# Attention's second projection moved to the end of its step, and VectorE's late copy moved ahead of the second maximum

## What is computed

```
dq = rope(rms_norm(dq.reshape(B, T, DA_HEADS, 2, DA_DK), lp['g_qn']), pos)
dk = rope(rms_norm(dk.reshape(B, T, DA_HEADS, 2, DA_DK), lp['g_kn']), pos)
s = einsum('bqhmd,bkhmd->bhmqk', q, k) * (DA_DK ** -0.5)      # two maps m per head
p = softmax(where(mask, s, min))
a = p[:, :, 0] - lam * p[:, :, 1]
o_d = rms_norm(einsum('bhqk,bkhe->bqhe', a, v), lp['g_dnorm']) * (1.0 - lam_init)
```

## Time and profile before

| | |
|---|---|
| median of 3 runs | 2151.39 us (2151.34 to 2151.40) |
| the profiled execution: its time | 2156.33 us |
| its span | 2154.5 us |
| TensorE busy | 2142.9 us, 99% |
| VectorE busy | 1161.8 us, 54% |
| ScalarE busy | 846.9 us, 39% |
| GpSimd busy | 505.6 us, 23% |
| attention loop | about 480 to 1037 us from the span's start |

### The profile page before, as it was taken

One profiled execution on the slowest core, in us unless ns is written; L12 is line 12 of the kernel. 1 busy time (PEld: TensorE's weight loads), 2 busy tenths in 40 slices (PEclk: granted clock), 3 DMA queues, 4 the chain that ended last, 5 costly groups with the idle time before them and its releaser, 6 DMA issues.

```text
span 2154.5 us, 34910 instructions
## 1 busy us (share of the span) xinstructions
PE 2142.9 (99%) x13462; PEld 2025.9 (94%) x13462; DVE 1161.8 (54%) x2354; ACT 846.9 (39%) x1951; POOL 505.6 (23%) x276
## 2 busy tenths in 40 slices
PE   9999999999999999999999999999999999999999
PEld 9999877789899898998999999999999999999999
DVE  6211544456636556366135648888988982322432
ACT  5200333335546566465312124444344353434411
POOL 5422201230040400501350510000000007576520
PEclk9999999999999999999999999999999999999999
DMA  8522223230040310402942421222222267666211
GB/s 272 199 84 89 62 69 102 78 107 25 26 124 30 89 57 29 122 28 65 325 154 73 149 89 40 82 76 74 90 80 70 80 195 237 189 183 192 88 43 51
DMA packets 319908, 227.18 MB, mean 105 GB/s; under 512 B 17402, under 2 KB 310892, under 8 KB 319757
## 3 DMA queue, kind: packets, MB, share of 16 engines
q1 hardware_dynamic: 222106, 119.68, 19.2%
q10 hardware_dynamic: 97650, 105.46, 14.5%
HBM read 164.47 MB, written 60.62 MB: 104 GB/s over the span
## 4 chain that ended last, share of the span: by engine, by line
PE 95%; issue 1%; DVE 1%; DMA 1%; ACT 1%; POOL 0%; ACTq 0%; DVEq 0%; POOLq 0%
PE ps L838 27%; PE ps L839 27%; PE ps L840 27%; PE ps L1126 3%; PE ps L1102 3%; PE ps L979 1%; PE ps L978 1%; PE ps L1117 1%; PE ps L1049 1%; PE ps L1054 1%; PE ps L1262 1%; PE ps L1051 1%; PE ps L1067 0%; PE ps L1278 0%; POOL w_all L812 0%
## 5 line engine op out<-in xcount | busy, mean ns | idle before, releaser
L838 PE MATMUL ps<-a_hi,w_all 128*128 128x352 f32 (+1 forms) x1360 | 415.6, 306 | 4.8 <-DVE a_lo L2700 4.0
L840 PE MATMUL ps<-a_hi,w_all 128*128 128x352 f32 (+1 forms) x1360 | 413.1, 304 | 0.0
L838 PE MATMUL ps<-a_hi,w_hi 128*128 128x352 f32 x1240 | 405.6, 327 | 0.0
L840 PE MATMUL ps<-a_hi,w_lo 128*128 128x352 f32 x1240 | 397.6, 321 | 0.0
L839 PE MATMUL ps<-a_lo,w_hi 128*128 128x352 f32 x1240 | 397.5, 321 | 0.0
L839 PE MATMUL ps<-a_lo,w_all 128*128 128x352 f32 (+1 forms) x1200 | 368.1, 307 | 0.0
L736 POOL TENSOR_SCALAR w_hi<-w_raw 128x1024 fp32r<-128x1024 f32 x92 | 100.8, 1096 | 967.3 <-DVE scr L2354 447.6
L838 PE MATMUL ps<-w_hi,a_hi 128*128 128x384 f32 (+1 forms) x768 | 286.4, 373 | 0.0
L840 PE MATMUL ps<-w_hi,a_lo 128*128 128x384 f32 (+1 forms) x768 | 273.4, 356 | 0.0
L839 PE MATMUL ps<-w_lo,a_hi 128*128 128x384 f32 (+1 forms) x768 | 272.8, 355 | 0.0
L838 PEld LDWEIGHTS ps<-a_hi,w_all 128*128 128x128 f32 x1360 | 256.1, 188 | 5.8 <-DVE a_lo L2700 4.3
(11 more groups left out here) (285 smaller groups left out, 3571.1 us busy)
## 6 DMA issues: line engine op xcount, KB each, us to landing
w_raw<-w_in SPq DMA_DIRECT2D x64, 512.0 KB, 4.3
w_raw<-w_down SPq DMA_DIRECT2D x48, 512.0 KB, 3.8
raw_half<-w_up SPq DMA_DIRECT2D x80, 256.0 KB, 3.0
hid_d<-scr ACTq DMA_DIRECT2D x22, 512.0 KB, 2.7
w_raw<-w_down SPq DMA_DIRECT2D x24, 384.0 KB, 3.8
scr<-gates_d ACTq DMA_DIRECT2D x24, 352.0 KB, 6.2
gates_d<-full ACTq DMA_DIRECT2D x13, 528.0 KB, 2.6
xt_d<-full ACTq DMA_DIRECT2D x1, 4224.0 KB
```

The costliest lines, as they stand in the source:

```text
L838: pe.matmul(out, lhs[0], rhs[0], start=start, stop=False)
L840: return pe.matmul(out, lhs[1], rhs[0], start=False, stop=stop)
```

## The change

In TensorE's step the second projection of tile `now`, with its waits, moves from behind the second scores to the end of the step, behind the three groups of transposes and late multiplications. In VectorE's step the copy of the late probabilities moves ahead of the memset and the maximum of the second map, so it stands directly behind the rotation. No instruction is added or removed.

```
--- before
+++ after
@@ TensorE, one step @@
                     scores(1, i).then_inc(S["s1_done"], 1)
-                if now:
-                    h, i, n = now
-                    if i == 0:
-                        pe.wait_ge(S["w_split"], 8 * h + (U_DIFF + 7))
-                        if h:
-                            wait_piece(pe, h - 1, 3, S["gate_ev"])
-                        else:
-                            pe.wait_ge(S["gate_ev"], GATE_PIECES)
-                    if n == 1:
-                        pe.wait_ge(S["ot_ev"], RET_TILES)
-                    project(2 * (i % 2) + 1, i, PB_SLOT, PB_SLOT + 3).then_inc(S["pb_done"], 1)
                 if fill:
                     h, k = fill
                     gate_fill(h, 2 * k + 1)
...
                     last.then_inc(S["dot_tr"], 1)
+                if now:
+                    h, i, n = now
...
+                    project(2 * (i % 2) + 1, i, PB_SLOT, PB_SLOT + 3).then_inc(S["pb_done"], 1)
@@ VectorE, one step @@
                 if normed and not turned:
                     inverse_of_sum(*normed)
+                if weighed and 4 <= weighed[1] < LAST:
+                    h, i, n = weighed
+                    dve.wait_ge(S["at1_tr"], h * 4 + (i - 3))
+                    dve.tensor_copy(a_t[:, 4:i + 1, :],
+                                    ps[:, 4, 0:(i - 3) * P].rearrange("p (b n) -> p b n", n=P)).then_inc(S["at1_ev"], 1)
                 if scored:
...
                                       negate=True).then_inc(S["m1_done"], 1)
-                if weighed and 4 <= weighed[1] < LAST:
-                    h, i, n = weighed
-                    dve.wait_ge(S["at1_tr"], h * 4 + (i - 3))
-                    dve.tensor_copy(a_t[:, 4:i + 1, :],
-                                    ps[:, 4, 0:(i - 3) * P].rearrange("p (b n) -> p b n", n=P)).then_inc(S["at1_ev"], 1)
                 if scored and not short(scored[1]):
                     combine(scored)
```

More of the change, by code:

```diff
@@ L1280, in _ @@
                     last.then_inc(S["dot_tr"], 1)
+                if now:
+                    h, i, n = now
+                    if i == 0:
+                        pe.wait_ge(S["w_split"], 8 * h + (U_DIFF + 7))
+                        if h:
+                            wait_piece(pe, h - 1, 3, S["gate_ev"])
+                        else:
+                            pe.wait_ge(S["gate_ev"], GATE_PIECES)
+                    if n == 1:
+                        pe.wait_ge(S["ot_ev"], RET_TILES)
+                    project(2 * (i % 2) + 1, i, PB_SLOT, PB_SLOT + 3).then_inc(S["pb_done"], 1)
             for p in range(1, 72):
```

## The result

The changed kernel takes 2178.94 us (median of four runs, 2178.20 to 2179.31) against 2151.39 before: 27.5 us more, forecast 28.5. The ratio of the runs is 1.0119, with a 95% interval from 1.0106 to 1.0132, or 22.8 to 28.4 us; the two medians alone give 1.0128. Its profiled execution took 2178.91 us with a span of 2177.1.

What follows compares the result with a forecast made beforehand. TensorE bounds the attention loop without a gap; uncovered stalls of 6.2 us in steps 1-5 and 8 plus 1.2 in step 9 make 7.4 a head, 29.6 for four, less 1: 2151.4 + 28.5 = 2180; forecast 2174-2186 (0.68), range 2167-2192.

Steps and rivals of the forecast that it cites:

- The bound: Attention loop: PE runs without a gap, so a head costs its matmuls and removing a wait returns almost nothing.
- The cover and the slack: Second projection (PB, 24 matmuls) ahead of the turned tile's transposes: 4.19 us cover, 2.80 for tile 8; lateness beyond it stalls.
- wake and restart: Each stall: 0.05 us wake plus 0.10 for the first unhidden weight load, 0.15 together; bounds 0 and 0.3.
- Steps 1 to 4 and 8: Transposes of the turned tile: 1.89, 1.39, 0.94, 0.45 and 0.38 us late, each plus 0.15.
- step 1: Step projecting tile 1, without scores: chain from the second projection's end ready at 6.08 us against PE's 4.19, 1.89 late.
- step 5: Step projecting tile 5: rotation 0.26 us late for the transposes, plus 0.15; up to 0.2 a head off for ScalarE coming earlier.
- Step 9: First gate-only step: ScalarE's folded-rows copy starts 1.52 us later, PE's second scores 1.08 late, 1.2 with wake; bounds 0.4, 1.5.
- VectorE's part: Earlier late-probabilities copy: saves some 1.4 us in step 8, a little in step 7; costs 0.4 on a path with slack.
- rival 2: Wait returns elsewhere: steps 6 and 7 stall, or late maxima delay combination or operands; 2186 to 2200 us, chance 0.10.
- rival 1: Smaller stalls: chain up to 0.5 us shorter in five late steps; 2165 to 2174 us, about 2170, chance 0.12.
- rival 3: Clock falls to 1.2 GHz after the gaps of nearly 2 us in steps 1 and 2: 34 us, 2214, chance 0.03.
- PB joined to the next projection: Second projection beside the next first one saves an operand-kind change per step, 3.5 us: about 2147 us, faster, chance 0.03.

Runs made afterwards that it cites:

- VectorE's part alone: Kernel before with only the late-probabilities copy moved ahead of the second map's maximum, the second projection in its old place: 2152.51 us, ratio 0.9994.
- tiles 6 and 7 only: Changed kernel with the second projection at the step's end for tiles 6 and 7 alone, the other seven in the old place: 2151.76 us, ratio 0.9998.
- both mends: Changed kernel with 12 second-projection matmuls back in the old place and ScalarE's fold copy behind its table load and square sum: 2152.62 us, ratio 1.0002.
- before with the short rotation: Kernel before with attention's cosine multiplication done on one column only, so queries and keys are wrong: 2152.06 us, ratio 0.9999.
- TensorE's part alone: Changed kernel with the late-probabilities copy put back behind the second map's maximum: 2192.00 us, ratio 1.0176.

## Why the prediction was right, point by point

**The bound.** PE had no gap in the loop, so no edit of order could give anything. Three kernels of other orders (VectorE's part alone, tiles 6 and 7 only, both mends) and one with a shorter chain (before with the short rotation) ended within 0.1% of before, none below it beyond its interval.

**The cover and the slack.** The stall of a step is the cover lost less the slack, plus wake and restart. Steps 1 to 4 and 8 came out within 0.09 us each. In step 1 the chain from PB's end, not a slack, was the right thing to count: 1.96 us against 2.04. The sum was right by its terms, not by errors that cancel: 7.2 us a head, after what was taken off for step 5, against 6.91, and a shorter stall in the first head's step 1, put at 0.3 us, came out at 0.24. The 4.19 us of cover held too. Had PB covered 0.3 us less, steps 2 to 4 would have stalled 0.3 less each, about 1.2, 0.8 and 0.3 us (an estimate).

**Step 5 was mis-sized**: 0.41 in the list, 0.08 measured. The sum had taken off up to 0.2 for ScalarE's earlier start, and more came. Timelines of ACT and DVE of the kernel before, then of the changed kernel:

```profile
664.46 0.30 ACT L1731 ACTIVATE scr<-scr,u_last 128x4 f32<-128x4 f32 x1
...
664.09 0.55 DVE L2425 COPY full<-ps 128x384 f32<-128x384 f32 x1
664.79 0.18 DVE L2431 RECIPROCAL scr<-scr 128x4 f32<-128x4 f32 x1 [0.16 <-ACT scr L1731]
```
```profile
674.66 0.30 ACT L1731 ACTIVATE scr<-scr,u_last 128x4 f32<-128x4 f32 x1
...
675.83 0.55 DVE L2425 COPY full<-ps 128x384 f32<-128x384 f32 x1
676.29 0.17 DVE L2431 RECIPROCAL scr<-scr 128x4 f32<-128x4 f32 x1
```

In the changed kernel the roots are there at 674.96, 1.3 us ahead of the reciprocal; before, they ended at 664.76 and the reciprocal started at 664.79, 0.15 behind the end of VectorE's copy. Now VectorE starts it 0.09 ahead of that copy's end. These 0.24 us took the 0.26 late of the list away, and what was left is the wake.

**Wake and restart** were put at 0.15 us. In step 2 the rotation ends at 644.29 and the transposes start at 644.35, 0.06 behind; the stall is 1.51 and the lateness 1.39, so both together make 0.12. They make 0.13 and 0.12 in steps 3 and 4, but only 0.07 and 0.06 in steps 1 and 8. So the term was some 0.05 too large in each of these five stalls, and it was an estimate that nothing before the change could show.

**Step 9** was put at 1.08 and wake, 1.2 with them: measured 1.26, by the forecast engines in the forecast order. Taking ScalarE's copy out of its place gave 1.30 back.

**VectorE's part** was put at 1.4 us in step 8 "and a little in step 7". It is worth 3.20 us a head: 1.54 in step 8 and 1.69 in step 7, where the late copy had the second maximum ahead of it as well. I worked that out only for the experiment's expectation. This did not touch the sum, as the changed kernel has both parts.

**The rivals.** Stalls in steps 6 and 7 or at the operands (rival 2) did not come. The smaller stalls of rival 1 came in step 5 alone. The clock did not fall in the loop in any trace, though PE waited 1.5 us in the first head's step 1 and 1.8 us in that of each other head of the changed kernel; the last section has where it did fall. PB joined to the next projection saved nothing: steps 6 and 7 took 13.42 and 13.91 us against 13.38 and 13.94.

## What to carry to other kernels

Where one engine has no gap, every block of its queue is cover for the chains that end behind it. Before moving a block, list for each wait behind it how long the awaited product has been ready, and take off the block's length: what goes below zero is the price, step by step, and the rest of the move is free. The move has a second side: whoever waits for the moved block's result starts later, and so does all that stands behind that waiter in its queue, needed or not (ScalarE's table load and square sum here).

## What the runs showed of the hardware that I had not expected

The time of one and the same kernel goes from 2150.6 to 2157.5 us (the 50 runs of before beside the experiments). In the traces most of the difference lies in one wait far behind the loop: PE waits for the last rounded piece of the hidden layer. Its data comes back by DMA, ScalarE rounds it and VectorE subtracts the rounded part (L2700). The wait is 4.0 us in the trace of before, 3.9 with TensorE's part alone and with VectorE's part alone, and 1.4 to 1.8 in the other seven.

Most of what is longer is the subtraction itself: 2.1 us in the three traces with the long wait, 0.5 to 1.3 in the others. Timelines of POOL and DVE of before, then of the changed kernel:

```profile
1785.64 2.34 POOL L738 TENSOR_TENSOR w_all<-w_raw,w_all 128x1024 fp32r<-128x1024 f32 x1
1786.28 2.08 DVE L2700 TENSOR_TENSOR a_lo<-a_pre,a_hi 128x352 fp32r<-128x352 f32 x1 [5.43 <-ACT a_hi L1978]
```
```profile
1812.54 0.53 DVE L2700 TENSOR_TENSOR a_lo<-a_pre,a_hi 128x352 fp32r<-128x352 f32 x1 [4.61 <-ACT a_hi L1978]
1812.73 2.59 POOL L738 TENSOR_TENSOR w_all<-w_raw,w_all 128x1024 fp32r<-128x1024 f32 x1
```

In nine of the ten traces a GpSimd instruction is running when the subtraction starts, and each time the subtraction ends 0.36 to 0.43 us behind the end of that instruction. In the tenth (before with the short rotation) none is running, and it takes 0.53 us. So a start 0.8 us later against GpSimd's instructions, when GpSimd is in its long instruction (L738) and no longer in the short one ahead of it (L736, 1.04 us), costs 1.5 us more. No run took GpSimd's work away, so this is what ten traces agree on and not a tested cause.

With each of the three long waits TensorE's clock fell. Timeline of PE and stretches view of the kernel before:

```profile
1788.42 0.66 PE L838 MATMUL ps<-a_hi,w_all 128*128 128x352 f32 x1 [4.00 <-DVE a_lo L2700]
1788.88 0.49 PE L839 MATMUL ps<-a_lo,w_all 128*128 128x352 f32 x1
1789.17 0.49 PE L840 MATMUL ps<-a_hi,w_all 128*128 128x352 f32 x1
...
1791.49 0.32 PE L839 MATMUL ps<-a_lo,w_all 128*128 128x352 f32 x1
1791.65 0.32 PE L840 MATMUL ps<-a_hi,w_all 128*128 128x352 f32 x1
```
```profile
1784.00:1788.00 4.00, 0.42 (x3) 0.12 (x1) 1.72 (x1) 0.50 (x1) 3.90 (x3) 1.00 0.70 202
1788.00:1792.00 4.00, 3.58 (x14) 3.58 (x15) 1.41 (x3) 1.56 (x3) 0.26 (x1) 0.57 0.77 224
```

The same matmuls start 0.29 us apart instead of 0.16, at 1.2 GHz, until 1791.4; then the clock is back at 2.4. That costs some 1.4 us. From the start of the turned tile's last transposes to the end it took 1146.4 us in that trace of before and 1141.8 in that of the changed kernel. Of these 4.6 us, 2.4 are the longer wait, 1.4 the clock, and 0.8 a wait for GpSimd (L812) that only before has. This is why the profiled execution of before, at 2156.33 us, lay 4.9 above its median, and why the spans of the two profiles differ by only 22.6 us where the medians differ by 27.5. Leaving aside the last few us of the program, the clock fell in one more trace, that of both mends, after a wait of 1.8 us at the same place. In six traces a wait of 1.4 to 1.7 there left it at full speed, and so did, in three, the waits of 1.8 in the attention loop. So a gap of this length may cost the clock or not, and rival 3 was less far off than my chance of 0.03 had it. What decides between the two I leave open.
